# A transpose ahead of the values visits and an earlier place for the rotated copies, in a two-layer transformer block on one core

## The reference

```
z = x @ w_in                                  # split in 14 column groups
q, kv = latents (rmsnorm) @ w_uq, w_ukv       # mla: rotated parts by _rope
o_mla = dense_causal_attention(q, k, v)
o_fox = dense_causal_attention(f_q, f_k, f_v, with a cumulated log decay)
idx_logit = einsum('bqhe,bke->bqhk', i_q, i_k)     # index queries and keys
score = sum over heads of relu(idx_logit) * i_w    # then top 64 keys per query
o_dsa = attention of s_q over the selected s_k, s_v
merged = sum over branches of sigmoid(gate) * (o @ w_branch)
x = layernorm(alpha * x + merged @ w_out)
x = layernorm(alpha * x + conv_glu_ffn(x))
```

## Time and profile before

| what | value |
|---|---|
| median of 3 runs | 848.56 us (847.6 to 848.8) |
| the profiled execution's own time | 848.64 us |
| its span, first to last instruction | 846.9 us |
| PE busy | 830.5 us, 98% |
| DVE busy | 607.5 us, 72% |
| ACT busy | 463.2 us, 55% |
| POOL busy | 112.0 us, 13% |

### The profile page before, as it was taken

The page is one execution under the profiler, slowest core; times in us unless marked ns, Lnnn a source line. Parts: engine busy times, 40 slices in busy tenths (PEclk is TensorE's granted clock), DMA queues, the critical chain, the costliest instruction groups (busy, mean ns, idle before and its releaser), DMA issues.

```text
span 846.9 us, 15667 instructions
## 1 busy us (share of the span) xinstructions
PE 830.5 (98%) x6316; PEld 774.9 (91%) x6316; DVE 607.5 (72%) x1078; ACT 463.2 (55%) x699; POOL 112.0 (13%) x133
## 2 busy tenths in 40 slices
PE   7999999999999999999999999999999999999996
PEld 6898999999899999988889989998998999999885
DVE  5675688887786877765676559788887787777554
ACT  5655766573356655553447377666535465555430
POOL 1503910005400000000000056000070000000000
PEclk9999999999999999999999999999999999999999
DMA  9859543435578677475846694434457777764731
GB/s 305 238 128 278 174 143 108 139 118 182 160 199 214 191 196 198 163 229 178 264 128 163 141 300 151 131 119 151 147 155 202 189 203 200 199 187 150 241 119 50
DMA packets 190264, 150.98 MB, mean 178 GB/s; under 512 B 32652, under 2 KB 164336, under 8 KB 189936
## 3 DMA queue, kind: packets, MB, share of 16 engines
q1 hardware_dynamic: 181120, 143.09, 57.4%
q10 hardware_dynamic: 9072, 6.90, 3.0%
HBM read 148.63 MB, written 1.06 MB: 177 GB/s over the span
## 4 chain that ended last, share of the span: by engine, by line
PE 91%; DVE 4%; ACT 1%; issue 1%; DMA 1%; SPq 1%; DVEq 0%; ACTq 0%
PE ps L661 28%; PE ps L663 27%; PE ps L662 27%; PE ps L939 3%; PE ps L970 2%; PE ps L951 2%; DVE w_lo L1467 2%; DMA raw<-w_in 1%; ACT w_hi L1131 1%; PE ps L719 1%; ACT qm_t L1203 1%; PE ps L905 0%; PE ps L1036 0%; DVE km_t L1780 0%; DVE prob L1620 0%
## 5 line engine op out<-in xcount | busy, mean ns | idle before, releaser
L1467 DVE TENSOR_TENSOR w_lo<-raw,w_hi 128x2048 fp32r<-128x2048 f32 (+3 forms) x142 | 304.9, 2150 | 119.0 <-ACT w_hi L1131 118.8
L661 PE MATMUL ps<-xt_hi,w_hi 128*128 128x256 f32 x1232 | 346.5, 281 | 0.0
L662 PE MATMUL ps<-xt_lo,w_hi 128*128 128x256 f32 x1232 | 342.1, 278 | 0.0
L663 PE MATMUL ps<-xt_hi,w_lo 128*128 128x256 f32 x1232 | 342.1, 278 | 0.0
L1131 ACT ACTIVATE w_hi<-raw 128x2048 fp32r<-128x2048 f32 (+3 forms) x142 | 252.6, 1784 | 81.5 <-PE ps L663 75.6
L661 PEld LDWEIGHTS ps<-xt_hi,w_hi 128*128 128x128 f32 x1232 | 232.3, 189 | 3.3 <-issue 2.4
L662 PEld LDWEIGHTS ps<-xt_lo,w_hi 128*128 128x128 f32 x1232 | 232.6, 189 | 0.0
L663 PEld LDWEIGHTS ps<-xt_hi,w_lo 128*128 128x128 f32 x1232 | 232.3, 189 | 0.0
L661 PE MATMUL ps<-w_hi,ht_hi 128*128 128x512 f32 x176 | 68.6, 390 | 0.0
L663 PE MATMUL ps<-w_hi,ht_lo 128*128 128x512 f32 x176 | 68.5, 389 | 0.0
L662 PE MATMUL ps<-w_lo,ht_hi 128*128 128x512 f32 x176 | 68.5, 389 | 0.0
(11 more groups left out here) (239 smaller groups left out, 1273.3 us busy)
## 6 DMA issues: line engine op xcount, KB each, us to landing
raw<-ffn_w_up SPq DMA_DIRECT2D x88, 512.0 KB, 5.1
raw<-w_in SPq DMA_DIRECT2D x84, 512.0 KB, 5.4
raw<-ffn_w_down SPq DMA_DIRECT2D x32, 512.0 KB, 4.1
raw<-w_branch SPq DMA_DIRECT2D x24, 512.0 KB, 4.3
raw<-w_out SPq DMA_DIRECT2D x16, 512.0 KB, 4.6
raw<-ffn_w_down SPq DMA_DIRECT2D x24, 256.0 KB, 2.9
decay<-decay_rows ACTq DMA_DIRECT2D x2, 1024.0 KB, 8.5
ln_g<-ln_g ACTq DMA_DIRECT2D x4, 512.0 KB, 3.9
```

What stands on the lines that cost most here:

```text
L661: pe.matmul(dst, a_hi, b_hi, start=first, stop=False)
L662: pe.matmul(dst, a_hi, b_lo, start=False, stop=False)
L663: return pe.matmul(dst, a_lo, b_hi, start=False, stop=last)
L1467: ins = dve.tensor_tensor(panel_lo(l, p)[0:n, cols], panel_raw(l, p)[0:n, cols], panel_hi(l, p)[0:n, cols].bitcast(F32), ALU.subtract)
```

## The change

Two edits. In the values visits below slot 24, that is five a layer, PE now transposes the identity matrix into bank 7 ahead of the visit; nobody reads the result. On ACT, the two `iq_t` copies of the panel IQ move behind the key copies and the rotated copies.

```diff
@@ PE, the loop over slots
                     for g in fourth_slot_pairs(s, LAG_V):
+                        if s < SLOTS:
+
+                            pe.transpose(ps[:, B_QK, 0:P], ident[:], ident[:])
                         values(l, g)
@@ ACT, the loop over panels
-                    if p in (FQ_AT, FQ_AT + 1, IQ_AT, SQ_AT):
-                        features_out(l, p)
                     if p == IQ_AT:
                         copy_keys(l)
                         rope_out(l)
+                    if p in (FQ_AT, FQ_AT + 1, IQ_AT, SQ_AT):
+                        features_out(l, p)
                     if p == FK_AT:
                         decay_out(l)
```

## The result

The changed kernel takes 844.45 us (843.8 to 845.9, 8 runs), the one before, on the same chip, 848.71 (846.8 to 851.3, 8 runs): a ratio of 0.9946 with an interval of 0.9934 to 0.9958. The forecast was 844.3. The time is right, and the way to it is not: two terms of the sum were wrong by about 1.7 each, with opposite signs. That they cancel is luck.

What follows compares the result with a forecast made beforehand. The prediction took PE, on the chain of waits for 91% of the span, as the bound. From 848.64 it took 3.94 (stalls) and 1.62 (low clock), added 1.1 (transposes) and 0.1 (GpSimd): 844.3 us, range 842.9 to 847.0.

Steps and rivals of the forecast that it cites:

- The stalls (3.94 booked): PE's idle ahead of the first index product, gone in both layers by ACT's new order: 1.99 + 1.95 us saved.
- Started at 62.98 they end near 67.0: Layer 0, ACT: key copies' issues and rotated copies, 4.0 us long, moved earlier, so the weight split starts 3.6 earlier.
- the bank it frees is used again only in the feature panel after: The first `iq_t` copy, ending at 67.4, can wait longer: its bank is needed only after the latent key and value products.
- The rival of the held issue: ACT's key copy issues held to about 67.0 by the decay store; split only 0.9 earlier, 846.3 or 847.9 us; 11%.
- margin of 13 us: Key copies in layer 0, issued near 63.0 and 63.6, have until 76.6 to land, when the index product needs them.
- rival "slower": Key copies issued behind the store land late and PE waits for index keys: over 0.2% slower (850.3 us); 4%.
- The clock (1.62 booked): Low granted clock (0.50) behind layer 0's first index visit goes with the idle ahead of it: 1.62 us saved.
- The transposes (1.1 booked): Ten added PE transposes ahead of the values visits cost 0.10 to 0.11 each, 1.1 us in all.
- the rival's reason for free transposes: Each transpose takes the place of the 0.10 of changing array shape before a values visit: 843.2 us; 10%.
- this edit only costs: The array's drain before a values visit comes with or without a transpose ahead, so the transposes save nothing.
- GpSimd's 0.1: Layer 1: DVE comes 1.95 earlier for GpSimd's masked scores and waits 0.1 us, which may reach PE; booked once.
- the 55%: Chance given to the whole forecast: both stalls and the clock dip gone, about 1.1 paid, 843.6 to 845.2 us.

Runs made afterwards that it cites:

- experiment 1: The ten transposes alone added to the kernel before, ACT's order left as it was: 849.49 us, ratio 0.9993 to the kernel before.

## Why the prediction was right and wrong

**The stalls (3.94 booked) were mis-sized.** The step that failed is "Started at 62.98 they end near 67.0": it took the second key copy's issue at its old length, 0.7. It held ACT for 4.46 in layer 0 and 4.09 in layer 1. The index stalls gave 1.42 + 1.39, and the late first `iq_t` copy took 0.47 + 0.07 back, so 2.27, 1.67 less than booked. The reasoning behind it ("the bank it frees is used again only in the feature panel after") was sound only with the copy at 67.4.

**The rival of the held issue had the mechanism.** It put the split at 71.3 and the gain at 0.95 a layer; the split came at 71.39, and layer 0 gained 1.42 - 0.47 = 0.95 (layer 1 1.39 - 0.07 = 1.32). The mistake was to give it 11%. Its evidence was in the rows: SP held for 4.93 by the same store. What I set against it, an ACT issue of 0.39 at 71.08, stood behind the drain (the store, issued from 53.75 on, had landed by 67.4), and proved nothing of an issue inside it. Likewise the landings of 5.9 and 6.5 were of copies issued behind the drain; inside it they became 10.2 and 10.3. The margin of 13 us covered that, so the rival "slower" stayed away.

**The clock (1.62 booked) was right**: 1.63, against this execution of the kernel before, which had the low clock once. With ACT's edit the windows there show full clock in each profile, with experiment 1's old stall they don't. But experiment 1's profile, with the same two idles, has it in both layers, and the mean clocks above say that the kernel before had it there in many executions, and in two perhaps not at all. So the term was no fixed price.

**The transposes (1.1 booked) were priced right and summed wrong.** Each costs 0.11, as rows 10 said (ten 1.15, not the estimated 0.8; the bf16 product costs 0.07), and the visit is still 0.20 behind it: the change of shape isn't filled. So the rival's reason for free transposes is refuted, while its sign is right. The step that failed is "this edit only costs": the tiles behind the visits run 0.004 a product quicker, 0.10 over a tile of 24, and the quick pace lasts on through further tiles. From the first visit to the sixth the kernel gained 0.33 in layer 0 and 0.49 in layer 1, where 1.1 in all was to be lost. Of the 0.49 nearly 0.2 lie in the branch panel ahead of the sixth visit. The bookkeeping stopped at the visit's start, and so could not see it.

**The small terms.** GpSimd's 0.1 did not reach PE. A wait of layer 1 that went (0.21), the slower pace behind the sixth visit there (-0.57) and a shorter stall (0.26) were not in the sum. The -0.57 isn't put down to the transposes for sure: the pace ahead of the sixth visit differs between layers of one kernel, with them and without. In the changed kernel the Trainium skill's rule of the drain ("TensorEngine Tiling (Array Packing)", Key Properties) agrees with the 0.20 that is still paid behind each transpose.

In the sum: the stalls were booked 1.67 too high (3.94 against 2.27), and all the rest 1.76 too low (a gain of 0.42 against 4.45 - 2.27 = 2.18). With the stalls alone mis-sized the time would have been 846.0, still in the range, which reached as far as the held issue. The point forecast was met by luck, and the 55% for all its steps together was too much.

**Open.** What a held issue waits for isn't shown; ACT's first one in the drain passed in 0.52. What in the PE keeps the two paces apart isn't known. The runs show when the pace is kept at ten visits, and not why the sixth differs. Whether the clock falls by the length of the idle or by something else beside it wasn't tried: of two equal idles in the kernel before, one was followed by it.

## What to carry to other kernels

An issue of a transfer is an instruction like any other: before moving it earlier, look whether it lands in a stretch in which the DMA engines are clogged, and what is queued behind it; put the work that needs no transfer ahead of it. Store to memory in pieces larger than a word where the layout lets you: here pieces of 32 bytes instead of 4, an eighth as many, were worth as much as the best order. And when an instruction is added to a busy PE, read the pace of what follows for some tiles, since a price taken at its own start may be given back there.

## What the runs showed of the hardware

- A store of single words (two issues, 4 KB each) took 12.8 to 14.3 us to land (the median of the two, in the traces that show it), and between 60 and 68 all transfers together ran at 18 to 28 GB/s. ACT's first issue in that time took about 0.5, the second 4.1 to 5.8 in the kernels that issue it there, and SP's 4.5 to 6.8. With 32-byte pieces none of these was held.
- The same fp32r product of 128 x 128 by 256 columns runs at 0.113 or 0.118 a piece over whole tiles at full granted clock. It turned at each of the first five values visits of a layer when nothing was added ahead of them (30 of 30), stayed quick with one full-array instruction there (80 of 80), and turned at the sixth either way (24 of 24).
- An idle of 1.9 us ahead of the index visit was followed, in one layer of one trace and in both of another, by 3.4 us at a granted clock of 0.50 (1.2 GHz); the one of the kernel before lost 1.6. Idles of 0.5 to 0.7 there, and one of 1.59 at the panel SQ, were not.
